# Sixteen convolution chunks and twelve mixing chunks turned by VectorE's block transposes and GpSimd's DMA queue

## The reference, cut to what matters

```
# block 1, conv_ffn, D_FF = 2816, a causal convolution of width 3 along the tokens
u = causal_dwconv(h @ w_up, conv_w, conv_b)
g, up = jnp.split(u, 2, axis=-1)
return (jax.nn.silu(g) * up) @ w_down

# block 2, mixing stage
q, k, v, f_logit, xr, gr, g_attn, g_rnn = jnp.split(h @ w_in[l] + b_in[l], ...)
q, k = rms_norm_2(q), rms_norm_2(k)                   # per head, 8 heads of 128
y_attn = forgetting_attention(q, k, v, log_sigmoid(f_logit)) @ w_o_attn[l]
xr = causal_depthwise_conv(xr, conv_w[l], conv_b[l])  # width 4, along the tokens
yr = rg_lru(xr, ...) * gelu(gr)                       # a recurrence along the tokens
x = x + (sigmoid(g_attn) * y_attn + sigmoid(g_rnn) * (yr @ w_o_rnn[l])) @ w_out[l]
```

## Time and profile before

| | |
|---|---|
| median of 3 runs | 1863.47 us (1863.38 to 1864.08) |
| the profiled execution's own time | 1863.22 us |
| its span | 1861.4 us |
| TensorE busy | 1850.0 us, 99% |
| VectorE busy | 1238.5 us, 67% |
| ScalarE busy | 1061.4 us, 57% |
| GpSimd busy | 95.6 us, 5% |
| DMA | 361.89 MB, mean 194 GB/s |

### The profile page before, as it was taken

How to read it: one execution, slowest core, us unless ns; L and a number is a source line. 1 busy time by engine, 2 the same in 40 slices (tenths; PEclk the granted TensorE clock), 3 DMA queues, 4 the chain that set the end, 5 groups by cost and what they waited for, 6 DMA issues and landing times. The chain is left out here.

```text
span 1861.4 us, 24532 instructions
## 1 busy us (share of the span) xinstructions
PE 1850.0 (99%) x9552; PEld 1565.7 (84%) x9552; DVE 1238.5 (67%) x1807; ACT 1061.4 (57%) x1536; POOL 95.6 (5%) x163
## 2 busy tenths in 40 slices
PE   8999999999999999999999999999999999999999
PEld 7889998879999888888888888888888888888887
DVE  6868777677777755557876654665555788665555
ACT  6756555666555643468855544363535886546352
POOL 2000000000000001000010010101010001000100
PEclk9999999999999999999999999999999999999999
DMA  8445564537556567644555466676675446456664
GB/s 265 156 140 200 172 207 165 174 114 230 184 182 204 184 201 251 210 172 159 179 195 204 161 223 227 218 260 215 212 234 196 159 158 230 152 190 209 219 234 136
DMA packets 164493, 361.89 MB, mean 194 GB/s; under 512 B 7782, under 2 KB 20683, under 8 KB 163867
## 3 DMA queue, kind: packets, MB, share of 16 engines
q1 hardware_dynamic: 154400, 327.24, 51.8%
q0 software_dynamic: 9520, 32.89, 6.0%
q10 hardware_dynamic: 459, 0.20, 0.0%
HBM read 348.73 MB, written 11.58 MB: 194 GB/s over the span
## 5 line engine op out<-in xcount | busy, mean ns | idle before, releaser
L1335 ACT ACTIVATE w_hi<-raw 128x1024 fp32r<-128x1024 f32 x620 | 633.3, 1054 | 451.1 <-PE bank L515 192.6
L2089 DVE TENSOR_TENSOR w_lo<-raw,w_hi 128x1024 fp32r<-128x1024 f32 x620 | 733.9, 1223 | 196.1 <-ACT w_hi L1335 189.2
L513 PE MATMUL bank<-w_hi,r_hi 128*128 128x512 f32 x1344 | 531.3, 395 | 1.2 <-DVE r_lo L2113 0.6
L515 PE MATMUL bank<-w_hi,r_lo 128*128 128x512 f32 x1344 | 523.9, 390 | 0.0
L514 PE MATMUL bank<-w_lo,r_hi 128*128 128x512 f32 x1344 | 523.2, 389 | 0.0
L513 PEld LDWEIGHTS bank<-w_hi,r_hi 128*128 128x128 f32 x1344 | 252.4, 188 | 56.4 <-DVE r_lo L2113 2.4
L515 PEld LDWEIGHTS bank<-w_hi,r_lo 128*128 128x128 f32 x1344 | 252.3, 188 | 53.5
L514 PEld LDWEIGHTS bank<-w_lo,r_hi 128*128 128x128 f32 x1344 | 252.6, 188 | 50.0
L513 PE MATMUL bank<-w_hi,z_hi 128*128 128x512 f32 x656 | 258.9, 395 | 1.5 <-DVE z_lo L2089 0.7
L515 PE MATMUL bank<-w_hi,z_lo 128*128 128x512 f32 x656 | 255.7, 390 | 0.0
L514 PE MATMUL bank<-w_lo,z_hi 128*128 128x512 f32 x656 | 255.6, 390 | 0.0
(11 more groups left out here) (231 smaller groups left out, 1557.4 us busy)
## 6 DMA issues: line engine op xcount, KB each, us to landing
raw<-in_w_in SPq DMA_DIRECT2D x79, 1024.0 KB, 5.1
raw<-in_ffn_w_down SPq DMA_DIRECT2D x44, 1024.0 KB, 7.9
raw<-in_w_up SPq DMA_DIRECT2D x40, 1024.0 KB, 5.2
raw<-in_ffn_w_gate SPq DMA_DIRECT2D x40, 1024.0 KB, 5.6
raw<-in_ffn_w_up SPq DMA_DIRECT2D x40, 1024.0 KB, 8.1
raw<-in_w_down SPq DMA_DIRECT2D x22, 1024.0 KB, 4.8
raw<-in_w_out SPq DMA_DIRECT2D x16, 1024.0 KB, 5.1
by_block<-qk POOLq DMA_DIRECT2D x20, 512.0 KB, 3.3
```

Source lines behind the costliest of these rows:

```text
L513: pe.matmul(out_, lh, rh, start=start, stop=False, skip_group_check=True)
L515: return pe.matmul(out_, ll, rh, start=False, stop=stop, skip_group_check=True)
L1335: A_(w_hi[:, n % NH, :], raw[:, u % NS, HALF * h:HALF * (h + 1)], ACT.Copy).then_inc(hi_ready, 1)
L2089: return V.tensor_tensor(dst, src, hi.bitcast(F32), ALU.subtract)
```

## The change

1. **Block 1's convolution, steps 0 to 3, gate and up** (8 chunks a layer, 16 in all): `quarter` takes the place of `quarter_rows`. ScalarE stages the banks (`gu_stage`, with the factor rstd), VectorE transposes 32x32 blocks (`gu_turn`), GpSimd's queue writes 512 KB to DRAM and reads it back in four pieces (`tokens_moved`), ScalarE copies it into `stage` (`unfold`). VectorE's `scale` is dropped for these chunks.
2. **Block 2's mixing stage, chunks 0 to 5** (6 a layer, 12 in all): `turned(n)` leaves TensorE; VectorE's `turn_chunk` and GpSimd's `chunks_moved` carry the chunk, and `store` reads it from SBUF. Chunks 6 and 7 stay on TensorE.
3. **Orders.** In `ffn_conv`, gate(j+1) now comes ahead of down(j-1), with the weight units in that order (`conv_units`); the hand-written lists of TensorE, ScalarE and VectorE are rewritten in both stages. The weights loaded are the same.

```diff
+    return ((0, 2, None), (4, 6, 10), (8, 12, 16), (14, 18, 22), (20, 24, 26), (28, 28, 30))[j]
...
+            def chunks_moved(l):
+                for n in range(6):
+                    pool.wait_ge(prod_turned, 2 * chunk_at(l, n) + 2)
+                    pool.dma_start(by_block[n % 2], chunk_blocks[n]).then_inc(prod_out, 16)
+                    pool.wait_ge(prod_out, 16 * (chunk_at(l, n) + 1))
+                    if 0 < n < 5:
+                        pool.wait_ge(qk_ready, 8 * LAYERS + 16 * l + 2 * n)
+                    if n == 5:
+                        pool.wait_ge(lru_conv, 4 * l + 4)
+                    for a in range(4):
+                        pool.dma_start(chunk_moved[n][32 * a:32 * a + 32, :]..., by_block[n % 2]...).then_inc(prod_in, 16)
+            def tokens_moved(f):
+                for j in range(4):
+                    for up in range(2):
+                        n = gu_at(f, j, up)
+                        pool.wait_ge(gu_turned, 2 * n + 2)
+                        pool.dma_start(by_token[n % 2], gu_blocks).then_inc(gu_out, 16)
+                        pool.wait_ge(gu_out, 16 * (n + 1))
+                        if n:
+                            pool.wait_ge(unfolded, 2 * n)
+                        for a in range(4): ...
...
-                    quarter_rows(u0 + ffn_units(j)[up] + i // 2, i // 2, i % 2, (A, B)[up],
-                                 None if j or up else KT * norm_at(where, n), free)
+                    (quarter if j < 4 else quarter_rows)(
+                        u0 + conv_units(j)[up] + i // 2, i // 2, i % 2, (A, B)[up],
+                        *((r_hi, r_lo) if j < 4 else ()), None if j or up else KT * norm_at(where, n), free)
...
+                def gu_stage(j, up, t): ...    # ScalarE: gu <- bank * rstd
+                def unfold(j, up, b): ...      # ScalarE: stage <- gu_moved, waits for gu_in
+                def gu_turn(j, up, t): ...     # VectorE: V.transpose(gu_blocks, gu)
+                def turn_chunk(n, t): ...      # VectorE: V.transpose(chunk_blocks[n], staged(n))
```

More of the change, by code:

```diff
@@ L1230, in _ @@
                 part(4, 3)
+                lru_linear(1)
                 part(5, 0)
-                turned(3)
                 part(5, 1)
@@ L1538, in ffn_conv @@
[L1538 to L1562, removed]
+                hi(u0 + 11, 0)
@@ new lines, in ffn_conv @@
+                main(3, 0, 1)
+                hi(u0 + 21, 0)
+                silu(3, 0)
+                hi(u0 + 21, 1)
+                gu_stage(3, 1, 0)
+                silu(3, 1)
+                gu_stage(3, 1, 1)
+                hi(u0 + 22, 0)
+                hi(u0 + 22, 1)
+                hi(u0 + 23, 0)
+                hi(u0 + 23, 1)
+                hi(u0 + 24, 0)
+                unfold(3, 1, 0)
+                unfold(3, 1, 1)
+                hi(u0 + 24, 1)
+                main(3, 1, 0)
@@ new lines, in ffn_conv @@
+                lo(u0 + 18, 1)
+                taps(2, 1, 0)
+                lo(u0 + 19, 0)
+                taps(2, 1, 1)
+                lo(u0 + 19, 1)
+                product(2, 0)
+                product(2, 1)
+                lo(u0 + 20, 0)
+                prod_lo(2, 0)
+                lo(u0 + 20, 1)
+                prod_lo(2, 1)
+                taps(3, 0, 0)
+                lo(u0 + 21, 0)
+                taps(3, 0, 1)
+                lo(u0 + 21, 1)
+                gu_turn(3, 1, 0)
@@ new lines, in ffn_conv @@
+                gu_turn(3, 1, 1)
+                lo(u0 + 22, 0)
+                lo(u0 + 22, 1)
+                lo(u0 + 23, 0)
+                lo(u0 + 23, 1)
+                scale(4, 0, 0)
+                scale(4, 0, 1)
+                lo(u0 + 24, 0)
+                lo(u0 + 24, 1)
+                taps(3, 1, 0)
+                lo(u0 + 25, 0)
+                taps(3, 1, 1)
+                lo(u0 + 25, 1)
+                product(3, 0)
+                product(3, 1)
+                lo(u0 + 26, 0)
@@ new lines, in ffn_conv @@
+                prod_lo(3, 0)
+                lo(u0 + 26, 1)
+                prod_lo(3, 1)
+                taps(4, 0, 0)
+                taps(4, 0, 1)
+                lo(u0 + 27, 0)
+                lo(u0 + 27, 1)
+                scale(4, 1, 0)
+                scale(4, 1, 1)
+                lo(u0 + 28, 0)
+                taps(4, 1, 0)
+                taps(4, 1, 1)
+                lo(u0 + 28, 1)
+                product(4, 0)
+                lo(u0 + 29, 0)
+                product(4, 1)
@@ L2992, in _ @@
                 lru_scan(2)
-                lru_low(2)
                 lo(u + 17, 0)
                 lo(u + 17, 1)
+                scale(5)
+                lru_low(2)
                 lo(u + 18, 0)
+                turn_chunk(5, 0)
+                turn_chunk(5, 1)
+                stage_chunk(7, 0)
                 sums(6)
-                stage_chunk(7, 0)
                 lo(u + 18, 1)
                 stage_chunk(7, 1)
-                copy_v(0, 0)
+                lru_gains(3)
                 lo(u + 19, 0)
```

714 lines of the change are left out of this document (451 added, 263 removed).

## The result

The changed kernel takes 1888.8 us (median of 4 runs, 1886.7 to 1891.7); the kernel before, run beside it, takes 1863.8. The ratio is 1.0133, with a 95% interval of 1.0121 to 1.0145: slower by 25 us, where 16 us faster was forecast. The profiled execution took 1886.7.

A forecast was written before the change was run, and what follows sets the result against it. TensorE, busy 1850.0 of 1861.4 us, was taken as the bound: 1861.4 - 10.2 - 10.8 + 5 of stalls = 1845.4 span, 1847.5 us in all. Range 1844.5 to 1851 (chance 0.40); 8 in 10: 1841 to 1857.5.

The forecast's parts named there:

- TensorE's terms: Convolution and mixing stage: wider matmuls and dropped transposes together shorten TensorE's stream by 21.0 us.
- The form of a chunk: Convolution: 48 matmuls of 512 columns replace 96 of 256, saving 0.64 us a chunk, 10.2 us for 16.
- the rival in which that saving isn't there: Convolution: 512 columns cost twice 256, so 10 us are missing and the kernel takes 1857 us; chance 0.05.
- `turned`: Mixing stage: each transpose step taken off TensorE saves 0.90 us; twelve leave, 10.8 us.
- So no stall in the convolution with round trips below 15: Convolution: TensorE never waits for late weights while a trip through memory stays under 15 us.
- the trip of 12.5 us: Both stages: a chunk's way to memory and back takes 10.4 to 15.0 us, taken as 12.5.
- the count of slack: Convolution: weights for up(2) are ready at 69.5 us and asked for at 72.0, 2.5 us of slack.
- the round trip sets the pace of the convolution: Convolution: `unfold` delays a `hi` in each of 16 chunks; trips of 16.5 us give 1878.5 us; chance 0.08.
- quarter 2 of chunk 6: Mixing stage: TensorE waits 2.0 us here for unit 13's weights, asked for at 80.7 us and ready at 82.7.
- VectorE becomes the bound in the mixing stage: Mixing stage: added block transposes fill VectorE, costing 11 us of stalls, 1853.5 us; chance 0.17.
- VectorE, ScalarE, the weight loads: Both stages: added work hides behind TensorE; VectorE reaches 88% in the mixing stage, ScalarE 68% in the convolution.
- My own marks: Signs of error: TensorE idle past 20 us, ScalarE's waits past 2 us a chunk, much later weight loads; trips expected 11 to 14.

The follow-up runs named there:

- e4: Changed kernel, but in the convolution ScalarE's `unfold` waits only for the turned chunk and reads a constant tile, all transfers kept: 1857.6 us, 0.9963.
- e12: Changed kernel, one buffer, work reordered ahead of the round-trip waits in both stages, including chunk 5's `store` behind other work: 1852.0 us, 0.9934.
- e8: Changed kernel, but each weight load of the two convolutions fetches a quarter of its bytes, instructions and waits the same: 1858.1 us, 0.9969.
- e6: Mixing part alone, with `lru_root(0)` ahead of `store(1, 0)` on ScalarE and both `lo` of unit 13 moved ahead on VectorE: 1859.6 us, 0.9975.
- e11: Mixing part alone, original orders, but `store` of chunks 0 to 3 reads a constant tile without waiting for the trip: 1856.7 us, 0.9965.
- e5: Changed kernel, with weights moved ahead of the up chunks' `unfold` and taps in convolution steps 1 to 3: 1886.9 us, 1.0130.

## Why the prediction was wrong

**TensorE's terms were right.** The form of a chunk: 5.0 us a convolution in e4, 5.1 predicted; the rival in which that saving isn't there is out. `turned`: 253.0 - 247.7 = 5.3 us of TensorE's time a stage in e12, 5.4 predicted. So the saving on TensorE's stream is real; the stalls and the clock behind them ate it. (The formula that the prediction took from the Trainium skill, "TensorE: Matmul & The Clock Gate", section "Back-to-back issue gap", is given there for an isolated matmul, not for a stream. The runs decide for the trace's 0.120 and 0.227 us.)

**The step that failed** is "So no stall in the convolution with round trips below 15", with the trip of 12.5 us that it rested on. Two things were wrong in it.

First, the size of the trip. It was 15.0 and 15.6 us at the two longest stalls of the first convolution, the top of my range. I had argued that the convolution's traffic would be like the feed-forward's, and the mean is alike. But a feed-forward's way out took 0.56 + 3.15, at a DMA share of 0.68; the two ways out ahead of those stalls (from 215.2 and from 253.2) took 5.3 us each at a share of 0.99. In all, GpSimd stood 3.9 to 8.6 us behind the 0.56, and e8 shows that it is the weight loads beside it. More rows of the feed-forward would not have helped: all 20 ways out there landed in 2.9 to 3.9 us. It was the wrong stage to take them from.

Second, the count of slack. It failed even where the trip was as short as I took it: TensorE waited 1.1 us for lo(u+13, 1) and 1.4 for lo(u+15, 1), behind trips of 12.0 and 11.7 us.

```profile
178.61 0.70 DVE L2481 STREAM_TRANSPOSE v<-v 128x512 f32<-128x512 f32 x1
191.28 1.16 ACT L1575 ACTIVATE stage<-qk 128x512 f32<-128x512 f32 x2 [0.61 <-DMA qk<-by_token]
200.59 0.50 PE L587 MATMUL bank<-w_hi,r_hi 128*128 128x512 f32 x1 [1.14 <-DVE w_lo L2276]
```

Counted from TensorE's first gate quarter (126.8 here), up(1) was turned by 52.5 us, where I had 48: the first trip of all, 15.1 us, had held VectorE up until 159.3, and from there to that turn it worked with only 0.8 us of idle time; my count let it start step 1 on time. That ate the slack of 2.5. And I stopped at units 13 and 15, as if later steps repeated them; the stalls of 2.9 and 2.8 us came in steps 2 and 3, behind the up chunks. A trip in step 2 starts late, because by the order `gu_stage(2, 1)` stands between two `silu`, and these behind the taps of a gate chunk that had itself been waited for. Lateness is handed from trip to trip: an order that holds for one round isn't shown to hold for the next.

**The rival that came true** is the third, "the round trip sets the pace of the convolution", to which I gave 0.08. Its mechanism was right: `unfold` ahead of a `hi`, with weights behind it. Its price was counted another way, 1 us for each us over 15 at 16 places, so it too had nothing below 15; TensorE stalled six times in the first convolution, for 9.2 us in all, at trips of 11.7 to 15.6 us, lost 3.4 more to the clock, and the remaining 1.9 of 14.5 us I can't place by a row.

**The mixing stage.** The place was right, quarter 2 of chunk 6, with 3.4 us for 2.0, and 0.9 us before it at chunk 5, where I had 0.9 of slack. The round trip of chunk 1 was 13.0 us (863.3 to 876.3), near the 12.5. Stalls and clock together made 6.2 and 7.2 us a layer instead of 2.5, by stage length less 253.2 - 5.4 = 247.8. The rival "VectorE becomes the bound in the mixing stage" priced this nearly right (5.5 a layer) for a wrong reason: e6 and e11 shorten the stage by 3.7 to 5.7 us with VectorE's work as it was. The rule of the Trainium skill that I set beside it ("VectorE: DVE Perf Modes", section "Rules for kernel authors": a 128x128 transpose goes to TensorE where PSUM will do as destination) is not borne out here as a matter of engine time: with the mixing part alone and the order of e6, VectorE carries the transposes and the kernel is 0.25% faster (0.9964 to 0.9985). (The 0.66% of e12 hold the saving of the convolution's form as well.) What they cost is the way to memory and back, and where it blocks.

**The clock** was in no term. The earlier trace rows show it full before, where past the first 6 us no wait of TensorE for another engine was longer than 0.6 us; here five stalls were followed by 1.7 us of loss each, 8.5 in all.

**VectorE, ScalarE, the weight loads.** All hidden, as said: e4 had all three as in the changed kernel. The loads did land later, 6.4 us for 5.2 (w_up), and 6.9 in e4, without harm.

My own marks worked: TensorE idle over 20 us (42.0), ScalarE's waits for moved blocks over 2 us a chunk (28.8 / 8 = 3.6), trips outside 11 to 14.

## What to carry to other kernels

An engine that works in order turns the latency of a transfer into a stall for everything queued behind the wait. When a step gets a trip through memory, put ahead of its wait all that doesn't depend on it and can already run, on every engine in the chain, and at every such wait: mended at the up chunks alone it gained under 3 us here (e5), at the gates too, with the next chunk sent off ahead of the wait, 27 in the two convolutions (200.9 and 202.1 to 188.1 and 188.3). Take the length of a transfer from rows where the same other transfers run beside it, not from a stage of the same mean traffic. And count slack with the lateness that the trips before have left, through the whole period of a loop until it repeats, not to the first tight place.

## What the hardware showed that I had not expected

A 512 KB transfer took 2.9 us from issue to landing with light weight loads beside it, and 4.2 to 8.9 (median 5.3) with full ones, though the DMA engines were busy for 66% of the convolution. The share in its own stretch doesn't set it alone: 5.3 us went with 99%, the 8.9 with 70%. The clock did not fall after each stall: it fell after one of 1.9 us at 515.1, and stayed full after 2.9 and 2.8 us at 554.6 and 592.3 in the same convolution. What decides it these runs do not show; the length of the stall alone doesn't.
